# Nineteen more 128-row blocks turned by VectorE and ScalarE instead of TensorE

## What is computed

```python
def first_block(x, ...):                       # one layer
    h = h + _gla_mixer(_rmsnorm(h, gla_norm[j]), ...)     # gated linear attention, 4 heads
    h = h + _sq_relu_mlp(_rmsnorm(h, mlp_norm[i]), mlp_w_up[i], mlp_w_down[i])
    return _rmsnorm(h, final_norm)

def second_block(x, mem, ...):
    h = h + hybrid_mixer(rmsnorm(h, norm_mix[l]), ...)    # delta rule, sliding window, stick breaking; gated and merged, @ w_o
    h = h + memory_cross_attention(rmsnorm(h, norm_xattn[l]), rmsnorm(mem, norm_mem[l]), ...)
    h = h + conv_ffn(rmsnorm(h, norm_ffn[l]), w_up[l], ffn_conv[l], w_down[l])
    return rmsnorm(h, norm_final)
```

## Time and profile before

| | us |
|---|---|
| median of 3 runs | 2526.01 (2525.94 to 2526.09) |
| the profiled execution, its own time | 2526.63 |
| its span, first to last instruction | 2525.0 |
| TensorE busy | 2509.5 of 2525.0 |
| VectorE busy | 1433.6 |
| ScalarE busy | 1369.2 |
| GpSimd busy | 33.4 |
| granted TensorE clock, mean | 0.999 |

### The profile page before, as it was taken

One profiled execution on the slowest core, in us unless ns is written; L12 is line 12 of the kernel. 1 busy time (PEld: TensorE's weight loads), 2 busy tenths in 40 slices (PEclk: granted clock), 3 DMA queues, 4 the chain that ended last, 5 costly groups with the idle time before them and its releaser, 6 DMA issues.

```text
span 2525.0 us, 29716 instructions
## 1 busy us (share of the span) xinstructions
PE 2509.5 (99%) x12742; PEld 2076.9 (82%) x12742; DVE 1433.6 (57%) x1112; ACT 1369.2 (54%) x1630; POOL 33.4 (1%) x41
## 2 busy tenths in 40 slices
PE   9999999999999999999999999999999999999998
PEld 7887888888888888888878888888888888888887
DVE  5644555545545545567765665545465666646774
ACT  6544445736637547566463553434364588538863
POOL 0000000000000000000000000000000000000000
PEclk9999999999999999999999999999999999999999
DMA  7454455555555555545443445555654555555554
GB/s 278 172 199 165 155 210 193 186 197 194 190 199 187 196 194 191 189 175 185 154 153 137 161 152 198 185 200 184 257 192 171 181 195 189 193 190 200 186 197 150
DMA packets 68930, 472.35 MB, mean 187 GB/s; under 512 B 7864, under 2 KB 8304, under 8 KB 12864
## 3 DMA queue, kind: packets, MB, share of 16 engines
q1 hardware_dynamic: 66608, 460.62, 50.9%
q0 software_dynamic: 1312, 7.73, 0.8%
q10 hardware_dynamic: 880, 2.11, 0.2%
HBM read 468.33 MB, written 2.11 MB: 186 GB/s over the span
## 4 chain that ended last, share of the span: by engine, by line
PE 96%; DVE 1%; DMA 1%; ACT 1%; issue 1%; SPq 0%; POOL 0%; POOLq 0%; DVEq 0%; ACTq 0%
PE acc L522 31%; PE acc L523 30%; PE acc L524 30%; PE tp L542 1%; PE tp L819 0%; DMA onorm<-in_rows 0%; PE tp L752 0%; DMA w_raw<-in_stream 0%; DVE w_lo L1617 0%; SPq L409 0%; PE tp L691 0%; DVE cv L1852 0%; PE tp L700 0%; PE tp L557 0%; ACT w_hi L1064 0%
## 5 line engine op out<-in xcount | busy, mean ns | idle before, releaser
L1617 DVE TENSOR_TENSOR w_lo<-w_raw,w_hi 128x2048 fp32r<-128x2048 f32 x431 | 986.2, 2291 | 730.4 <-ACT w_hi L1064 728.3
L1064 ACT ACTIVATE w_hi<-w_raw 128x2048 fp32r<-128x2048 f32 x431 | 824.1, 1916 | 587.5 <-DMA w_raw<-in_stream 566.4
L522 PE MATMUL acc<-w_hi,x_hi 128*128 128x512 f32 (+1 forms) x2240 | 876.0, 391 | 2.0 <-DVE w_lo L1617 1.1
L523 PE MATMUL acc<-w_lo,x_hi 128*128 128x512 f32 (+1 forms) x2240 | 868.5, 388 | 0.0
L524 PE MATMUL acc<-w_hi,x_lo 128*128 128x512 f32 (+1 forms) x2240 | 868.4, 388 | 0.0
L522 PEld LDWEIGHTS acc<-w_hi,x_hi 128*128 128x128 f32 x2240 | 420.6, 188 | 91.8 <-issue 2.3
L524 PEld LDWEIGHTS acc<-w_hi,x_lo 128*128 128x128 f32 x2240 | 420.5, 188 | 86.5
L523 PEld LDWEIGHTS acc<-w_lo,x_hi 128*128 128x128 f32 x2240 | 420.8, 188 | 84.8 <-issue 1.0
L522 PE MATMUL acc<-w_hi,a_hi 128*128 128x512 f32 x1120 | 437.6, 391 | 0.0
L523 PE MATMUL acc<-w_lo,a_hi 128*128 128x512 f32 x1120 | 435.8, 389 | 0.0
L524 PE MATMUL acc<-w_hi,a_lo 128*128 128x512 f32 x1120 | 435.8, 389 | 0.0
(11 more groups left out here) (363 smaller groups left out, 1131.9 us busy)
## 6 DMA issues: line engine op xcount, KB each, us to landing
w_raw<-in_stream SPq DMA_DIRECT2D x431, 1024.0 KB, 4.8
w_raw<-in_stream SPq DMA_DIRECT2D x12, 256.0 KB, 7.4
h<-in_x SPq DMA_DIRECT2D x4, 512.0 KB, 14.5
frow<-in_rows POOLq DMA_DIRECT2D x2, 1024.0 KB, 7.1
m_raw<-in_mem_turned POOLq DMA_DIRECT2D x1, 2048.0 KB, 10.2
memt<-in_mem POOLq DMA_DIRECT2D x1, 2048.0 KB, 19.2
x_raw<-in_x_turned SPq DMA_DIRECT2D x3, 512.0 KB, 8.0
dec<-gc_rows ACTq DMA_DIRECT2D x1, 1024.0 KB, 6.2
```

What stands on the lines that cost most here:

```text
L522: pe.matmul(dst, xh, wh[:, k], start=first and k == 0, stop=False)
L523: pe.matmul(dst, xh, wl[:, k], start=False, stop=False)
L1064: act.activation(w_hi[:, c % SLOTS], w_raw[:, c % SLOTS], ACT.Copy).then_inc(hi_ready, 1)
L1617: dve.tensor_tensor(w_lo[:, c % SLOTS], w_raw[:, c % SLOTS], w_hi[:, c % SLOTS].bitcast(F32), ALU.subtract).then_inc(lo_ready, 1)
```

## The change

Nineteen blocks leave `transposes`: four of the GLA queries and keys (`gT` 0 to 3), the outputs of heads 0 to 2 (`yT`), all four quarters of norm 1, quarters 0 to 2 of norm 3, the four merged blocks (`mT`), and quarter 3 of norm 6. They are turned in one of three ways.

- `block_turned` (the four `gT`): 16 DVE transposes of strips of 32x256 that read `nat` and write straight to the right partitions of `qT` or `kT`, eight before and eight after a weight split.
- `carried`: one DVE transpose of 128x1024 and 16 ACT strips, eight in one chunk's turn and eight in the next, then the high part on ACT and the low part on DVE out of SBUF (`ym`, `sq` or `mm`).
- For the last block of a chain (norm 1 quarter 3, merged 3, norm 6 quarter 3) ACT carries eight strips and DVE carries the other eight at the same time (`half_carried`).

Beside that, `EARLY` becomes 4; ACT waits for the small gate weights alone (`wg_in`) and not for all of GpSimd's first transfers; `stats` of norms 1 and 3 moves one turn later; the DVE product of the last value block (`("vN", 5)`) moves from turn 27 to turn 26 of the mixer; and chunk 11 of stage X is computed row block by row block, with the order of the eight products after it changed.

```diff
-    EARLY = 3
+    EARLY = 4
...
         @block.tensor
-                    if c == 37 + 4 * hd:
+                    if hd == 3 and c == 37 + 4 * hd:
                         tps.wait(pe, tps.name[("o", hd)])
                         transposes(tps.name[("yT", hd)], sr[:, :, hd * N:(hd + 1) * N])
...
-                if c in (8, 9, 12, 16):
-                    n = (8, 9, 12, 16).index(c)
-                    accs.wait(pe, accs.name[("gla", n)])
-                    transposes(tps.name[("gT", n)], nat[:, n % 2])
...
-                if c in (5, 9, 13):
-                    norm_part(1, c // 4 - 1)
...
                     if g == 0 and c < 4:
-                        tps.wait(pe, tps.name[("norm", 1, c)])
+                        pe.wait_ge(b_low, SIDE["norm1", c] + 1)
...
-                    elif j == 1:
-                        pe.wait_ge(mg_ready, 2 * nb)
-                        transposes(tps.name[("mT", nb - 1)], mg[(nb - 1) % 2])
...
+                if c < 11:
+                    chunk(C_X + c, X if b == 1 else A, 4 * q, accs.name["xk"] + b, q == 0, q == 3)
+                else:
+                    chunk(C_X + c, A, 4 * q, accs.name["xv"], False, True, rows_=(0,), done=False).then_inc(first_rows_done, 1)
+                    chunk(C_X + c, A, 4 * q, accs.name["xv"], False, True, rows_=(1,))
...
-            pe.wait_ge(xv_ready, 1)
-            for hd in range(4):
-                for b in range(2):
-                    mm = pe.matmul(tp[:, g % 2, hd], xv[:, b, hd * P:(hd + 1) * P], xpT[:, :, hd, b], start=b == 0, stop=b == 1)
+            for hd, b in ((0, 0), (2, 0), (0, 1), (1, 0), (1, 1), (2, 1), (3, 0), (3, 1)):
+                if (hd, b) == (0, 1):
+                    pe.wait_ge(xv_ready, 1)
+                mm = pe.matmul(tp[:, g % 2, hd], xv[:, b, hd * P:(hd + 1) * P], xpT[:, :, hd, b], start=b == 0, stop=b == 1)
...
-                    if g == 0 and c == 0:
-                        norm_part(6, 3)
...
         @block.scalar
+            def carried(name, dst, src, quadrants):
+
+                if 0 in quadrants:
+                    act.wait_ge(b_turned, SIDE[name] + 1)
+                src = src.rearrange("p (m k s j) -> p m k s j", m=M, k=4, s=4)
+                dst = dst.rearrange("p k (m q j) -> p m k q j", m=M, q=4)
+                for q in quadrants:
+                    for to in range(4):
+                        ins = act.activation(dst[32 * to:32 * to + 32, :, :, q], src[32 * q:32 * q + 32, :, :, to], ACT.Copy)
+                if 3 in quadrants or name in LAST:
+                    ins.then_inc(b_moved, 1)
+                    act.wait_ge(b_moved, SIDE[name] + 1)
+                if name in LAST:
+                    act.wait_ge(b_half, LAST[name])
+
+            def norm_last(j, src, dst, gains):
+                carried((f"norm{j}", 3), dst, src, (0, 1))
+                for q in range(4):
+                    t = 12 + q
+                    ins = act.activation(x_hi[:, t], dst[:, q], ACT.Copy, scale=col[:, gains + t:gains + t + 1])
+                ins.then_inc(b_high, 1)
...
-            turned_high(3)
-            split(3)
-            act.wait_ge(gla_in, 96)
+            act.wait_ge(wg_in, 16)
             act.activation(wg[:, :, 0:16], wg_raw[:], ACT.Copy).then_inc(wg_h, 1)
             for c in range(64):
+                if c == 4:
+                    act.wait_ge(gla_in, 80)
...
+                if c - 48 in (4, 8, 12):
+                    norm_carried(1, (c - 48) // 4 - 1, 0, COL["mlp_norm"])
                 if c - 48 in (5, 9, 13):
-                    high(1, (c - 48) // 4 - 1, COL["mlp_norm"])
-                    stats(1, (c - 48) // 4 - 1)
+                    norm_carried(1, (c - 48) // 4 - 1, 1, COL["mlp_norm"])
                 if c:
                     split(c + AHEAD)
+                if c - 48 in (6, 10, 14):
+                    stats(1, (c - 48) // 4 - 1)
...
         @block.vector
+            def half_carried(name, dst, src):
+
+                dve.wait_ge(b_turned, SIDE[name] + 1)
+                src = src.rearrange("p (m k s j) -> p m k s j", m=M, k=4, s=4)
+                dst = dst.rearrange("p k (m q j) -> p m k q j", m=M, q=4)
+                for q in (2, 3):
+                    for to in range(4):
+                        ins = dve.tensor_copy(dst[32 * to:32 * to + 32, :, :, q], src[32 * q:32 * q + 32, :, :, to])
+                ins.then_inc(b_half, 1)
...
+            def block_turned(n, quadrants):
+
+                src = nat[:, n % 2].rearrange("p m (k s j) -> p m k s j", k=4, s=4)
+                dst = (qT if n < 2 else kT)[:, 4 * (n % 2):4 * (n % 2) + 4].rearrange("p k (m q j) -> p m k q j", m=M, q=4)
+                for q in quadrants:
+                    for to in range(4):
+                        ins = dve.transpose(dst[32 * to:32 * to + 32, :, :, q], src[32 * q:32 * q + 32, :, :, to])
+                if 3 in quadrants:
+                    ins.then_inc(q_turned, 1)
+
...
-                if c in (8, 9, 12, 16):
-                    n = (8, 9, 12, 16).index(c)
-                    g = tps.name[("gT", n)]
-                    dve.wait_ge(tp_done, g + 1)
-                    dst = (qT if n < 2 else kT)[:, 4 * (n % 2):4 * (n % 2) + 4].rearrange("p k t -> p (k t)")
-                    dve.tensor_copy(dst, tpf(g)).then_inc(tps.sem(g), 1)
+                if c in (8, 10, 12, 24):
+                    n = (8, 10, 12, 24).index(c)
+                    accs.wait(dve, accs.name[("gla", n)])
+                    block_turned(n, (0, 1))
+                    split(c + AHEAD)
+                    block_turned(n, (2, 3))
...
-                if c == 24 or c == 27:
+                if c == 24 or c == 26:
                     b = 4 if c == 24 else 5
                     g = tps.name[("vN", b)]
...
             for c in range(4):
                 add_to_h(("xo", c), c, last=C_XO + c)
+                if c == 3:
+                    accs.wait(dve, accs.name[("xo", 3)])
+                    dve.transpose(fturned[1][:].rearrange("p (m n) -> p m n", m=M), h[:, :, 3 * N:]).then_inc(b_turned, 1)
+                    half_carried(("norm6", 3), fm[1][:], fturned[1][:])
                 if c:
                     low_x(6, c - 1, COL["norm_ffn"])
```

More of the change, by code:

```diff
@@ L377, in build @@
         add(("ydnT", 0), ("ydnT", 1))
-        for nb in range(NB):
-            add(("mT", nb))
         for c in sorted(WO_PARTS):
@@ L387, in build @@
         add("xo_")
-        add_norm(6)
+        for n in range(3):
+            add_quarter(6, n)
         add(*[("fvT", g) for g in range(2)])
@@ L1460, in _ @@
                 if c == 1:
-                    g = tps.name[("mT", 3)]
-                    take(g, flat(m_hi[:, 12:16]), tpf(g), 0.5, m_half)
+                    act.wait_ge(b_low, SIDE["merged", 2] + 1)
+                    carried(("merged", 3), mm[:], mturned[:], (0, 1))
+                    act.activation(m_hi[:, 12:16], mm[:], ACT.Copy, scale=0.5).then_inc(b_high, 1)
                 if c in MEM_PARTS:
@@ L1574, in _ @@
                         product_high(part, 3)
+                    if part == 0 and c == 0:
+                        norm_last(6, fturned[1][:], fm[1][:], COL["norm_ffn"])
                     if not (q == 1 and 1 <= b < 8):
@@ L1650, in low_x, with norm_turned, norm_low @@
                 ins.then_inc(tps.sem(g), 1)
+            def norm_turned(j, n, name):
+                k = SIDE[f"norm{j}", n]
+                accs.wait(dve, accs.name[name])
+                if n >= 2:
+                    dve.wait_ge(b_moved, k - 1)
+                dve.transpose(turned[n % 2][:].rearrange("p (m n) -> p m n", m=M), h[:, :, n * N:(n + 1) * N]).then_inc(b_turned, 1)
+            def half_carried(name, dst, src):
[6 more added lines that the diff above has]
+                ins.then_inc(b_half, 1)
+            def norm_low(j, n, gains, src=None):
+                src = sq[n % 2] if src is None else src
+                dve.wait_ge(b_high, SIDE[f"norm{j}", n] + 1)
+                for q in range(4):
+                    t = 4 * n + q
+                    ins = dve.scalar_tensor_tensor(x_lo[:, t], src[:, q], col[:, gains + t:gains + t + 1], x_hi[:, t].bitcast(F32),
+                                                   ALU.mult, ALU.subtract)
+                ins.then_inc(b_low, 1)
             def normed_rows(j, n, gain_row, done):
@@ L1780, in _ @@
                         accs.wait(dve, blk)
+                        if part == 0 and n == 0:
+                            dve.wait_ge(b_moved, SIDE["norm1", 3] + 1)
                         if 4 * part + n >= 2:
```

246 lines of the change are left out of this document (149 added, 97 removed).

## The result

| us | before | after |
|---|---|---|
| median | 2526.05 (6 runs, 2525.92 to 2526.41) | 2507.6 (6 runs, 2507.14 to 2507.77) |
| profiled execution, its own time | 2526.63 | 2507.65 |
| its span | 2525.0 | 2505.6 |
| TensorE busy | 2509.5 | 2493.0 |

The ratio is 0.9926, interval 0.9914 to 0.9939: 18.5 us less.

The account below looks back on a forecast made before the run. The prediction took a full TensorE as the bound. Its terms, 16.9 + 2.4 + 1.4 + 0.6 - 0.5 = 20.8 us, led to a forecast of 2505.5 us, own range 2503.5 to 2508, 8 in 10 range 2503.5 to 2512.

Parts of the forecast that it names:

- What bounds the kernel: Whole kernel: TensorE is busy 2509.5 of 2525.0 us, so what leaves its queue shortens the time if nothing becomes late.
- 19 x 0.89 = 16.9: TensorE's queue: each of the 19 transpose blocks costs 0.89 us in line, so removing them gains 16.9 us.
- gT and chunk 16: GLA, three gT blocks in turns 8 to 12: VectorE's queue makes weight chunk 16 late by 0.5 us.
- Rival A: Helper engines' cover thinner than replayed: chunk 16 1.7 us late, feed-forward chunk 3 about 0.3; 2507 to 2512 us; chance 0.14.
- The seams: OUT/MLP, merged 3 and XO seams: the added work fits, with 0.7 and 0.4 us left at XO; cost nothing.
- The added start: Kernel start: waits for weight chunk 3 and the gate weights shrink, 2.4 us gained, bounds 0.8 and 2.6.
- vN 5: Mixer, last value block: its VectorE product goes ahead of chunk 29's split, so TensorE's 1.4 us wait goes.
- xv: Stage X, products ahead of XO: two products fill the 1.0 us wait for xv; 0.6 gained, bounds 0 and 1.0.
- Rival B: Start, vN 5 and xv: the gains only move into other waits, 4.4 less 0.5 lost; about 2509.5 us; chance 0.11.
- Rival C: VectorE strips cost as much as whole tiles, 1.245 us: slower, 2543 us, decided from about 0.82 per strip; chance 0.03.

Follow-up runs that it names:

- Experiments 3: The changed kernel with the four gT blocks 0 to 3 put back on TensorE, the other 15 staying off: 2508.97 us.
- 8: The changed kernel with block gT 2 turned at turn 20 and the cross-attention keys turned by VectorE: 2504.34 us; also with x fetched by one transfer: 2503.79 us.
- Experiment 7: The changed kernel with ScalarE carrying all sixteen strips of the three last quarters: 2513.12 us, repeated 2512.07; with ScalarE carrying twelve and VectorE four: 2508.51 us.
- experiment 1: The changed kernel with the early start, vN 5 and xv edits undone and the 19 blocks kept off TensorE: 2511.34 us.
- experiment 6: The changed kernel with every strip transpose of the four gT blocks done twice: 2532.39 us, ratio 1.0022 to the kernel before.

## Why the prediction was right

**What bounds the kernel** held: TensorE is full, and what leaves its queue leaves the time unless a chunk is late. Experiments 3 and 8 add and remove blocks and find 0.8 to 0.9 for each.

**19 x 0.89 = 16.9** was measured as 0.80 in one chunk and 0.09 in the next at nearly every place (0.88 at once at the three heads, 0.66 and 0.10 at gT 3), 16.9 in all. The busy time fell by 16.5.

**gT and chunk 16** was the term of the sum that was mis-sized: -0.5 forecast, -1.86 measured. The mechanism, the chunk and the order of steps were right. The failed step is the price: "Back-to-back DVE operations overlap (...), so I take 0.37 per strip". I had read the overlap from four `x_lo`, whose operations are longer and of another kind, and laid it on the strips. The strips don't overlap at all: 0.446 from start to start, which is the line through the two DVE transposes of the earlier trace rows (0.445) with nothing taken off. Two of the halves lie behind chunk 14's high part and are 0.6 longer each: 1.2 of the 1.36. The Trainium skill's formula ("VectorE: DVE Perf Modes", section "The TRN2 errata"), which it states for a float32 addition, gives 424 ns per strip. With nothing hidden that would have made an estimate of 1.3, the nearer value; the measurement is 436 ns per strip.

**Rival A**, the thinner cover, was therefore half true: 0.445 per strip and chunk 16 late by 1.7 is what happened, and the time, 2507.6, lies in the overlap of A's range and the forecast's. Its other half, 0.42 for a copy and chunk 3 of the feed-forward late, did not come.

**The seams** held, helped by one price that was too high: the DVE strip copy takes 0.30 and not 0.34 (eight 2.38, forecast 2.8). The changed kernel's timeline at the XO seam answers to the earlier trace rows:

```profile
1973.98 1.22 DVE L1749 TENSOR_TENSOR h<-acc,h 128x1024 f32<-128x1024 f32 x1
1975.23 1.25 DVE L2297 STREAM_TRANSPOSE fturned<-h 128x1024 f32<-128x1024 f32 x1
1976.51 2.38 DVE L1725 COPY fm<-fturned 32x256 f32<-32x256 f32 x8
1978.93 1.66 DVE L1706 SCALAR_TENSOR_TENSOR x_lo<-tp,col,x_hi 128x256 fp32r<-128x256 f32 x4
1980.51 2.28 DVE L1675 TENSOR_TENSOR w_lo<-w_raw,w_hi 128x2048 fp32r<-128x2048 f32 x1
...
1987.16 1.67 DVE L1734 SCALAR_TENSOR_TENSOR x_lo<-fm,col,x_hi 128x256 fp32r<-128x256 f32 x4
```

Chunk 2's low part is there 1.1 us before TensorE wants it (0.7 forecast). `x_lo` of quarter 3 ends at 1988.8 against 1989.3: 0.5 left (0.4 forecast). Experiment 7 shows how thin that is: four strips more on ScalarE and 1.1 us are lost.

**The added start** was put at 2.4. The trace up to chunk 4 shows 2.7 and 0.1 more in chunk 4, the undone edit 1.4 by the medians: 0.7 to 0.8 is given back at the end of the span and outside it, and the wait for `wg` varies between executions (1.0 to 1.5). The prediction compared its sum with the profiled execution's own time as if what lies around the span stayed as it was; it did not.

**vN 5** gave 1.46 (1.4 forecast) and **xv** 0.54 (0.6). **Rival B** fell with experiment 1: the waits were not replaced by others, though 0.8 of the start's gain was lost elsewhere. **Rival C** said that strips at the price of whole tiles would make the kernel slower, from about 0.82 per strip. At 0.89 it is slower, by 6 us (experiment 6). Only this one price was measured, so the point of turning itself was not. And part of the loss is the clock, which the rival's sum did not have: without the two low stretches that kernel would be at about 2527.8, an estimate, less than 0.1% above before. A point of turning somewhat below 0.89 fits that.

From 2505.5: 1.4 for chunk 16, 0.8 for the two ends, less 0.4 for a start that gained more in the trace than forecast, gives 2507.3 against 2507.6. So the total was closer than its terms by some luck: without the start's extra 0.4 it would have stood at the very end of the forecast's own range. And the ends, which the sum left out, cost more than half as much as the mis-sized strips.

## What to carry to other kernels

When one engine is full and others have a few us of delay free per stage, what counts for moved work is not its sum but how much of it stands between two fixed points: behind the last input that the helper waits for and ahead of the step that the full engine needs. Price small back-to-back operations from a row of their own kind, start to start, and where none is there take no overlap off. Spread them over turns before making them cheaper: one number changed gave 1.8 us here (2.0 by the trace), a cheaper way to turn gave 1.3 (1.1 by the trace).
